# Attention scores of block 1 as three fp32r products of high and low parts

## The reference, cut to what matters

```python
# stick breaking, per head and block of 128 queries
z = jnp.einsum('bhqd,bhkd->bhqk', q_blk, k) * d ** -0.5
log_beta = jax.nn.log_sigmoid(z)
log_1mb = jnp.where(strict, jax.nn.log_sigmoid(-z), 0.0)
between = lax.cumsum(log_1mb, axis=3, reverse=True) - log_1mb
a = jnp.where(strict, jnp.exp(log_beta + between), 0.0)
# differential attention, per head and block of 128 queries
logits = jnp.einsum('bhmqd,bhmkd->bhmqk', q_blk, k) * scale + bias
p = jax.nn.softmax(jnp.where(rel >= 0, logits, -jnp.inf), axis=-1)
w = p[:, :, 0] - lam * p[:, :, 1]
```

## Time and profile before

| | |
|---|---|
| median of 3 runs | 2822.18 us (2819.12 to 2822.81) |
| the profiled execution | 2822.24 us |
| its span in the profile | 2820.4 us |
| instructions | 38224 |
| PE busy | 2723.1 us (97%) |
| DVE busy | 1648.4 us (58%) |
| ACT busy | 859.5 us (30%) |
| POOL busy | 1596.2 us (57%) |

### The profile page before, as it was taken

One profiled execution on the slowest core, in us unless ns is written; L12 is line 12 of the kernel. 1 busy time (PEld: TensorE's weight loads), 2 busy tenths in 40 slices (PEclk: granted clock), 3 DMA queues, 4 the chain that ended last, 5 costly groups with the idle time before them and its releaser, 6 DMA issues.

```text
span 2820.4 us, 38224 instructions
## 1 busy us (share of the span) xinstructions
PE 2723.1 (97%) x13138; PEld 2180.2 (77%) x13138; DVE 1648.4 (58%) x2348; ACT 859.5 (30%) x1696; POOL 1596.2 (57%) x1242
## 2 busy tenths in 40 slices
PE   7999999899999999999999999989999999999998
PEld 5677777676878888887788887767787878888887
DVE  5666687738467777777734303484445446556556
ACT  4555445535312112114422114554233100100102
POOL 3555511455987777765523243222366987777764
PEclk9999999999999999999999999999999999999999
DMA  3322321034111111124411342213424021111134
GB/s 137 102 89 83 94 94 53 16 137 153 57 45 60 53 45 59 52 82 160 179 45 45 89 145 98 74 61 108 159 97 157 31 68 45 59 52 45 59 126 143
DMA packets 76777, 243.75 MB, mean 86 GB/s; under 512 B 7119, under 2 KB 10992, under 8 KB 76276
## 3 DMA queue, kind: packets, MB, share of 16 engines
q1 hardware_dynamic: 54576, 184.31, 20.0%
q10 hardware_dynamic: 22084, 57.86, 5.8%
HBM read 207.00 MB, written 32.52 MB: 85 GB/s over the span
## 4 chain that ended last, share of the span: by engine, by line
PE 81%; DVE 8%; POOL 5%; ACT 3%; issue 2%; DMA 0%; POOLq 0%; ACTq 0%; DVEq 0%
PE ps L817 16%; PE ps L819 16%; PE ps L818 16%; PE ps L1129 7%; PE ps L1130 7%; PE ps L1131 7%; PE ps L901 2%; PE ps L917 2%; POOL arena L707 1%; PE ps L1412 1%; PE ps L1424 1%; PE ps L932 1%; DVE ps L2492 1%; DVE ps L2509 1%; DVE ps L2533 1%
## 5 line engine op out<-in xcount | busy, mean ns | idle before, releaser
L640 POOL CAST wh<-raw 128x1024 fp32r<-128x1024 f32 x175 | 187.3, 1070 | 842.0 <-PE ps L819 799.0
L817 PE MATMUL ps<-hh,wh 128*128 128x512 f32 x1456 | 598.4, 411 | 8.1 <-DVE hl L2453 3.6
L819 PE MATMUL ps<-hh,wl 128*128 128x512 f32 x1456 | 571.1, 392 | 0.0
L818 PE MATMUL ps<-hl,wh 128*128 128x512 f32 x1456 | 569.9, 391 | 0.0
L642 POOL TENSOR_TENSOR wl<-raw,wh 128x1024 fp32r<-128x1024 f32 x175 | 421.9, 2411 | 14.0
L733 POOL TENSOR_TENSOR wl<-raw,wh 128x512 fp32r<-128x512 f32 x256 | 344.3, 1345 | 20.5
L817 PEld LDWEIGHTS ps<-hh,wh 128*128 128x128 f32 x1456 | 275.6, 189 | 79.1 <-issue 20.7
L819 PEld LDWEIGHTS ps<-hh,wl 128*128 128x128 f32 x1456 | 274.4, 188 | 59.9
L818 PEld LDWEIGHTS ps<-hl,wh 128*128 128x128 f32 x1456 | 275.7, 189 | 52.5 <-issue 3.4
L817 PE MATMUL ps<-gated,wh 128*128 128x512 f32 (+1 forms) x728 | 279.7, 384 | 3.5 <-DVE gated L2543 3.2
L818 PE MATMUL ps<-gated,wh 128*128 128x512 f32 (+1 forms) x728 | 278.4, 382 | 0.0
(11 more groups left out here) (341 smaller groups left out, 5080.5 us busy)
## 6 DMA issues: line engine op xcount, KB each, us to landing
raw<-weights SPq DMA_DIRECT2D x271, 512.0 KB, 3.5
arena<-w_ada SPq DMA_DIRECT2D x48, 512.0 KB, 3.8
arena<-gate_scratch ACTq DMA_DIRECT2D x20, 512.0 KB, 5.2
arena<-x_t ACTq DMA_DIRECT2D x1, 4096.0 KB, 14.2
x_scratch<-arena ACTq DMA_DIRECT2D x2, 2048.0 KB, 8.4
arena<-x_scratch SPq DMA_DIRECT2D x2, 2048.0 KB, 10.2
gate_scratch<-arena ACTq DMA_DIRECT2D x16, 256.0 KB, 2.2
x_scratch<-arena ACTq DMA_DIRECT2D x1, 4096.0 KB, 13.6
```

Source lines behind the costliest of these rows:

```text
L640: pool.tensor_copy(wh[:, s], raw[:, r]).then_inc(Z.wt_hi, 1)
L817: pe.matmul(out, wh[:, slot, w], xh, start=start, stop=False)
L818: pe.matmul(out, wh[:, slot, w], xl, start=False, stop=False)
L819: return pe.matmul(out, wl[:, slot, w], xh, start=False, stop=stop)
```

## The change

1. The evictions of queries and keys (ACT, as before) write fp32r high parts; DVE computes the low parts as PSUM minus high, one instruction for each Q and K fill (512 columns) and one of 1024 columns each for job 0. It does so last in its step, after a wait for the eviction.
2. The scores of each chunk of keys are three fp32r products per side, high x high, high x low, low x high, accumulated in PSUM; the sides alternate. A chunk is at least 256 columns wide, so those of 128 are padded.
3. TensorE's waits before the scores of a job and before a fill that follows a Q or K fill on its bank are for the low part instead of the eviction.
4. The low parts need memory: T(12) and T(24) hold two of the queries' low parts, a new buffer of 3 x 1024 columns the others and the keys'. The modulation keeps one accumulator, T(14); its six groups are multiplied in steps 8 + 8g instead of 10 + 8g, and DVE waits for the multiplication of the group before when it begins a group.

```diff
+        low3 = place("low3", [P, 3, S], F32R)
+        qk = place("qk", [P, 4, S], F32R, ARENA_AT)
+        low_a = place("low_a", [P, S], F32R, ARENA_AT + 4 * 12 * S)
+        low_b = place("low_b", [P, S], F32R, ARENA_AT + 4 * 24 * S)
...
-        Q_T, K_T = [T(0), T(2)], [T(1), T(3)]
+        Q_HI, K_HI = [qk[:, 0], qk[:, 2]], [qk[:, 1], qk[:, 3]]
+        K_LO = [low3[:, 0], low3[:, 1]]
+        def q_lo(i):
+            return low3[:, 2] if i % 2 else (low_b[:] if i == JOBS - 2 else low_a[:])
...
-        MOD_IN, MOD_ACC = T(13), [T(14), T(12), T(14), T(12), T(14), T(24)]
+        MOD_IN, MOD_ACC = T(13), T(14)
...
+        def fill_low(n):
+            return 2 + 4 * (n // 6) + n % 6 + 1
...
-        MOD_AT = {10 + 8 * g: g for g in range(6)}
+        MOD_AT = {8 + 8 * g: g for g in range(6)}
...
                     if k == 0 and n >= 2:
-                        pe.wait_ge(Z.f_ev, fill_evicted(n - 2))
+                        if (n - 2) % 6 < 4:
+                            pe.wait_ge(Z.f_low, fill_low(n - 2))
+                        else:
+                            pe.wait_ge(Z.f_ev, fill_evicted(n - 2))
...
                 if s % NB == 0:
-                    pe.wait_ge(Z.f_ev, fill_evicted(6 * (i - 1) + 3) if i else 2)
+                    pe.wait_ge(Z.f_low, fill_low(6 * (i - 1) + 3) if i else 2)
+                parts = ((Q_HI[i % 2], K_HI[i % 2]), (Q_HI[i % 2], K_LO[i % 2]), (q_lo(i), K_HI[i % 2]))
                 for c in range(0, w, HALF):
-                    e = min(w, c + HALF)
-                    for side in range(2):
-                        r = slice(DH * side, DH * (side + 1))
-                        last = pe.matmul(bank(2 * side, 2)[:, c:e], Q_T[i % 2][r, query(s)], K_T[i % 2][r, c:e],
-                                         start=True, stop=True, skip_group_check=True)
-                        if e == w:
-                            last.then_inc(Z.z_full, 1)
+                    e = max(min(w, c + HALF), c + 2 * P)
+                    for n, (q, k) in enumerate(parts):
+                        for side in range(2):
+                            r = slice(DH * side, DH * (side + 1))
+                            last = pe.matmul(bank(2 * side, 2)[:, c:e], q[r, query(s)], k[r, c:e],
+                                             start=(n == 0), stop=(n == 2), skip_group_check=True)
+                            if n == 2 and e >= w:
+                                last.then_inc(Z.z_full, 1)
...
                 if k == 0:
-                    dve.tensor_scalar(MOD_ACC[g], MOD_IN, col("c", k), None, ALU.mult).then_inc(Z.mod_acc, 1)
+                    if g:
+                        dve.wait_ge(Z.t_full, T_AT["mod", g - 1] + 1)
+                    dve.tensor_scalar(MOD_ACC, MOD_IN, col("c", k), None, ALU.mult).then_inc(Z.mod_acc, 1)
...
+            def low_out(hi, lo, ps, scale):
+                if scale == 1.0:
+                    dve.tensor_tensor(lo, ps, hi.bitcast(F32), ALU.subtract).then_inc(Z.f_low, 1)
+                else:
+                    dve.scalar_tensor_tensor(lo, ps, scale, hi.bitcast(F32), ALU.mult, ALU.subtract).then_inc(Z.f_low, 1)
+            def fill_low_out(n):
+                i, kind, t = 1 + n // 6, n // 2 % 3, half_of(n % 2)
+                dve.wait_ge(Z.f_ev, fill_evicted(n))
+                hi, lo = ((Q_HI[i % 2], q_lo(i)), (K_HI[i % 2], K_LO[i % 2]))[kind]
+                low_out(hi[:, t], lo[:, t], bank(6 + n % 2), 1.0 if kind else DH ** -0.5)
...
+            for n, (hi, lo) in enumerate(((Q_HI[0], q_lo(0)), (K_HI[0], K_LO[0]))):
+                dve.wait_ge(Z.f_ev, n + 1)
+                low_out(hi, lo, bank(2 * n, 2), 1.0 if n else DH ** -0.5)
...
+                for n in fills_done(s):
+                    if n % 6 < 4:
+                        fill_low_out(n)
```

More of the change, by code:

```diff
@@ L181, in build @@
         n_sq n_sum n_ss n_ln n_rstd n_t n_hi n_lo f_ln f_rstd f_y f_x
-        f_half f_ev t_full t_free z_full pv_full o_ev
+        f_half f_ev f_low t_full t_free z_full pv_full o_ev
         mask_in s_mask s_reset s_u s_b s_c s_a d_near d_max d_nmx d_exp d_r d_m d_w
@@ L956, in modulation @@
                 for f in range(8):
-                    last = pe.matmul(bank(4)[:, f:f + 1], MOD_ACC[g][:, f * P:(f + 1) * P],
+                    last = pe.matmul(bank(4)[:, f:f + 1], MOD_ACC[:, f * P:(f + 1) * P],
                                      mat("mean")[:, 0:1], start=True, stop=True)
@@ L1731, in _ @@
             act.preload_act_table_set("sigmoid_and_others")
-            for n, dst in enumerate((Q_T[0], K_T[0], HVT)):
+            for n, dst in enumerate((Q_HI[0], K_HI[0], HVT)):
                 act.wait_ge(Z.chunk_done, C_QKV + n + 1)
@@ L1738, in fill_out @@
                 i, kind, half = 1 + n // 6, n // 2 % 3, n % 2
-                dst = (Q_T[i % 2], K_T[i % 2], HVT)[kind]
+                dst = (Q_HI[i % 2], K_HI[i % 2], HVT)[kind]
                 if half:
@@ L2592, in mod_add @@
                 if k == 0:
-                    dve.tensor_scalar(MOD_ACC[g], MOD_IN, col("c", k), None, ALU.mult).then_inc(Z.mod_acc, 1)
+                    if g:
+                        dve.wait_ge(Z.t_full, T_AT["mod", g - 1] + 1)
+                    dve.tensor_scalar(MOD_ACC, MOD_IN, col("c", k), None, ALU.mult).then_inc(Z.mod_acc, 1)
                 else:
                     dve.wait_ge(Z.mod_acc, n)
-                    dve.scalar_tensor_tensor(MOD_ACC[g], MOD_IN, col("c", k), MOD_ACC[g], ALU.mult, ALU.add).then_inc(Z.mod_acc, 1)
+                    dve.scalar_tensor_tensor(MOD_ACC, MOD_IN, col("c", k), MOD_ACC, ALU.mult, ALU.add).then_inc(Z.mod_acc, 1)
+            def low_out(hi, lo, ps, scale):
[8 more added lines that the diff above has]
+                low_out(hi[:, t], lo[:, t], bank(6 + n % 2), 1.0 if kind else DH ** -0.5)
             def mod_out(g):
@@ L3320 @@
     }
-    nc = bacc.Bacc("TRN2", target_bir_lowering=False, num_devices=1, dynamic_dma_scratch_size=1024)
+    nc = bacc.Bacc("TRN2", target_bir_lowering=False, num_devices=1, dynamic_dma_scratch_size=512)
     d = {n: nc.dram_tensor(n, v.shape, mybir.dt.from_np(v.dtype), kind="ExternalInput").ap() for n, v in arrays.items()}
```

## The result

The changed kernel takes 2841.4 us (median of 6 runs, 2836.0 to 2843.1) against 2820.7 us for the one before on the same chip, **20.7 us slower** by the medians; the ratio of the runs is 1.0069 (95% interval 1.0058 to 1.0079, which is 16 to 22 us). The forecast was 2820.9 with a range of 2811 to 2832, so the result lies outside it, on the slow side. The profiled execution took 2836.0 us, the lowest of the six, and its mean granted clock is, with 0.988, the highest of the six (down to 0.985): so its trace shows somewhat less of the loss than the others had.

The account below looks back on a forecast made before the run. TensorE was taken to bound the kernel, nearly full in the stick-breaking half of block 1's attention. Scores -8.9, low parts +1.0 and moved modulation +6.6 gave -1.3 us, so 2820.9 us, range 2811 to 2832.

Parts of the forecast that it names:

- Scores, -8.9: Attention scores on TensorE: three fp32r passes against four fp32 ones save 8.9 us over eight jobs.
- Low parts, +1: VectorE's low-part subtractions after the fills: mostly covered, charged 1 us for the softmax half, at most 8.
- Rival 2: Softmax half, steps 33 to 53: low parts make VectorE the bound and delay score steps; about 2830 us, 15%.
- The moved modulation, +6.6 within 0 to +12: Modulation moved to steps 8, 16, ... 48: TensorE waits there for VectorE's copy of the transposes; +6.6 us net.
- upper bound of +12: Moved modulation: +12 us if the 2.0 taken from steps 10 to 50 only uncovers VectorE's lateness there.
- Rival 1: Steps 8 to 48: the moved modulation costs little, later slack makes up the stalls; 2814.3 to near 2817 us, 27%.
- Rival 3: Scores: the two 64-row sides do not run beside each other in fp32r; +53 us, 2874, 8%.
- rival 4: Scores: three weight loads in place of two per side and chunk stand outside the products; +49 us, 2870, 4%.

Follow-up runs that it names:

- products left out: The changed kernel with one product of 8 columns in place of each modulation's eight one-column products, same place and waits: 2822.8 us, ratio 1.0013.
- wait filled: The changed kernel with 16 extra unread fp32r products of 384 columns ahead of each of the six moved modulations: 2829.6 us, ratio 1.0029.

## Why the prediction was wrong

**Scores, -8.9: right.** With the low parts' +1 the two were to give -7.9; measured by themselves they give -9.7 by the medians and -7.9 by the ratio, +/- 3. By width, start to start: 1.58 to 1.60 for 1024 keys (1.58 said), 1.42 for 896 (1.42), 1.24 for 768 (1.25), 0.88 for 512 (0.89), 0.72 for 384 (0.73), 0.55 for 256 and for padded 128 (0.56). Taking the pitch of a full-height stream for that of 64-row products held.

**Low parts, +1: right in size**, 0 as far as can be told (0.5 us between the medians with and without them, the other way). Each takes 0.68 us (0.69 said). Rival 2, VectorE as the bound of the softmax half, falls with that.

**The moved modulation, +6.6 within 0 to +12: this is the step that failed.** It measured +22.9 us in the kernel before; in the changed one, against the kernel with the scores alone, step 63 starts 26.7 later (+16.5 and -10.2). What the term named was there: TensorE idle for 2.87 us (2.5 said), step 24 longer by 4.4 (4 said), step 26 shorter by 1.95 (2 said). Of each three steps the lost clock is taken off, and what remains against the kernel with the scores alone is +1.6, +1.5, +1.4 for steps 8, 16 and 24 (1.5 each said), -0.6 for 32 (-1.1 said), +2.3 and +1.8 for 40 and 48 (1.6 each said): 8.0 us for 6.6. So the path was right within 1.4 us by the trace, within 4 by the rest of the move alone (+10.3). Added to it come the 17 us of lost clock (18 over all runs), which had no place in the sum: it priced an idle TensorE by the time it stands, and the work behind at its usual durations. The upper bound of +12 had the same gap. The profile of before gave the warning in one column: the 0.99 of its first half is the 3.4 us at half clock behind the modulation of step 10. Around step 24 TensorE is without a fill product for 4.0 us there; the change made that 9.8.

The Trainium skill has the rule that would have asked the question ("TensorE: Matmul & The Clock Gate", Part 1, "What's actually happening"): the throttled state is the default, and activity releases it. The trace agrees as far as half clock comes behind all six waits and is gone from there once fill products stand among the same work; but it also comes behind small work without any wait (153.40 in the kernel before, 3.30 of 3.30 us busy).

**Rivals.** Rival 1 (the move costs little) is what another place gives: with the modulation among the fills 4.5 us over the scores alone, with the copy first and no padding 0.3. In the order of the change it was false. Rival 3 (sides one after the other) falls by 1.60 us for 1024 keys, where it said 3.0; rival 4 (weight loads show) by the same row, where it said 2.5. The Trainium skill's rule named beside it, that a load overlaps running products only where the row group differs, is not borne out: loads of the same 64 rows lie under products, and the pitch stays 0.23.

**What stays open.** What exactly makes the clock fall is not settled. It fell behind waits of 2.9 us without the one-column products (products left out, though not in step 8), and behind 1.9 us of one-column products with thin work after them and no wait (wait filled, though not in step 32); with the same products among fills it fell behind none of the six. But the last rows of the table show stretches of 3.4 us with a fall and of 4.3 us without one, and nearly equal ones that differ. So the same place can go either way, and what decides it there no run shows. No run took both the wait and the one-column products away in the changed order.

## What to carry to other kernels

Where a change moves thin work (products of few columns, transposes) or a wait into one place on TensorE, add up how long the engine then goes without wide products, and look at the granted clock of that stretch and of the one behind it: here a wait of up to 3 us and 2 us of one-column products cost another 3 us of clock on the mean, behind the wait, where its engine looks fully busy. Price a move by its whole neighbourhood, and try the place between two wide products first; the same work among the next step's fill products made the kernel 26 us shorter. And when two edits come together, one of which only makes room for the other, run each alone: the gain of 8 to 10 us was real and buried under a loss of 23. Where every run's clock is on record, multiply it out: it told here, without a look at the timeline, that up to 18 of the 20.7 us were clock.

## What the runs showed of the hardware that was not expected

- The granted clock of TensorE falls to half (0.50, 1.2 GHz) in or behind a step's quiet end, for 3.3 to 10.1 us, also while the engine shows 100% busy (6.70 of 6.70 us). The kernel before has it too, for 3.4 us from 153.3 and again from 525.4.
- At half clock the scores of 128 keys, padded to 256 columns, take 0.94 us for 0.55, the values 1.90 for 1.10, and 16 one-column products with their loads 3.0 to 3.5 for 1.9: the small work slows down as the wide does.
- In the scores, where each pair of fp32r products brings new weights, pairs of 128 columns come no faster than pairs of 256 (0.12 us).
- Two fp32r streams of 64 rows run side by side as two fp32 ones do: 0.23 us for a pair of 512 columns, against 0.43 for a pair of fp32 instructions, of which it takes two.
